# Bank waits at the output and merge products, an earlier remainder at the second index unit, head weights turned 72 rows at once, and row sums of the spatial weights in two fp32r parts

## The chip, the cores and the metric

The kernel runs on one core of one Trainium2 chip. The metric is the device time of one execution in microseconds, the median of several runs. TensorE (PE) multiplies, VectorE (DVE), ScalarE (ACT) and GpSimd (POOL) work element by element, SyncE (SP) issues the weight loads. Each engine runs its own list of instructions in order and waits on semaphores that the others raise.

## The reference, cut to what matters

Two blocks run one after the other on x of 256 rows by 1024 columns, all in float32:

```python
# first block
h = _rmsnorm(x, norm_g)
u, v, za, ab, ab_gate, zb, g_a, g_b = split(h @ w_in + b_in)          # 8 parts of 1024 columns
v = (_normalize(gelu(v)) * a_ln_g + a_ln_b)
mixed = einsum('gij,bnjgc->bnigc', masked(a_ws), v) + a_bs            # a_ws: 8 groups of 128 x 128
y_a = gelu(u) * mixed * silu(za)
y_b = silu(groupnorm(conv31(ab * sigmoid(ab_gate)))) * silu(zb)
merged = sigmoid(g_a) * (y_a @ w_pa) + sigmoid(g_b) * (y_b @ w_pb)
x = x + merged @ w_out
x = x + sigmoid(_rmsnorm(x, ple_norm_g) @ w_ple_gate) * (p @ w_ple)
x = _rmsnorm(x, final_g)
# second block
qa, ka, va, qb, kb, vb, qi, ki, wi, xc, yc, gates = split(_rmsnorm(x) @ w_in_2)
score = sum_h wi[h] * relu(qi[h] . ki)                                # 8 index heads, ki has 64 columns, wi has 8
y_a, y_b, y_c = attention, attention over the 64 best keys by score, gated linear recurrence
merged = g0 * (y_a @ w_pa_2) + g1 * (y_b @ w_pb_2) + g2 * (y_c @ w_pc_2)
x = x + merged @ w_o_2
x = x + relu(_rmsnorm(x) @ w_up_2)**2 @ w_down_2
return _rmsnorm(x, final_norm_g_2)
```

The bias a_ln_b of the layer norm goes through the spatial product as well: what it adds to row i of group g is a_ln_b times the sum of row i of the masked a_ws. These are the row sums of the title.

## The kernel before, in words

**Units.** All weights are cut into 123 units of 1 MB (some smaller), numbered c in the order of the list UNITS, which is written out by hand. A unit lands in one of three slots (c modulo 3) of `raw`. ScalarE copies it, rounded, to `whi` (`hi(c)`, L519, fp32r), and the remainder `raw - whi` goes to `wlo` (`lo(c)`, L897 on VectorE; for c from 3 to 27 both halves on GpSimd, L462). A product is then three fp32r matmuls for each k tile: high by high, high by low, low by high (L1547 to L1549). The inputs are held as such pairs too: a_hi and a_lo, b_hi and b_lo, c_hi and c_lo. Each engine's code walks the units; in the turn c ScalarE does `hi(c + 1)` or `hi(c + 2)` and drains the unit before.

**Banks.** The products of unit c go to PSUM bank U[c % 3]; M[0] to M[3] are four other banks and M[4] is an eighth. A bank is free for the next unit when the drain of its last user is counted in `act_drained` or `dve_drained`. `drained_count(c)` is the value of that counter once unit c has been drained.

**The places of the change.**
- Row sums (L1687 to L1690). After unit 8, the first v unit, TensorE multiplies the masked, transposed spatial weights wsT (8 groups of 128 columns) by a tile of ones into M[2] and M[3], as two fp32 matmuls of 512 columns. VectorE clears the masked corner of wsT in its turn c == 8 (L1009 to L1011). The sums are used in its turn c == 10 (L1015).
- Output (L1772 to L1774). The pb units are 36 to 39, in banks U[0], U[1], U[2], U[0]. The unit out 0 (`rows_half`) writes its rows 0 to 127 to U[2] and its rows 128 to 255 to U[0]. Before it, TensorE waits until unit 39 has been drained.
- Index units (L1218, L1292 to L1312). The units are qi 50 and 51, ki 52, xc 53 and 54. They are drained multiplied by r_bc, the reciprocal norm of each row, which TensorE spreads over the partitions in the middle of unit 53 (`norm_broadcast`, L1790) and VectorE copies to SBUF (L1218). Behind that copy VectorE does: drain qi 0, `lo(54)`, drain qi 1, `lo(55)`, drain ki, `lo(56)`, drain xc 0. TensorE may begin unit 54 only when qi 1, in its bank, has been drained; the first index scores (`dots`, L1802) want xc 0 drained.
- Head weights (L1869). Rows 64 to 71 of the ki product are wi. VectorE copies these 8 rows to wiT, and TensorE turns them into columns of M[2].
- Merge and w_o (L1938 to L1943). pb2 1 is unit 84 in U[0], pa2 0 and 1 are 85 in U[1] and 86 in U[2]. The unit wo 0 writes U[0] and U[1]; wo 1 writes U[2] and M[4]. Before wo 0 TensorE waits for the merged high and low parts (`m2_lo`) and until unit 86 has been drained.

Of the kernel before, what the change touches and what calls it, by code (L numbers as in the profile page):

```python
# [24 lines left out]
P = 128  # L25
# [104 lines left out]
def block_program(nc, I, onehot, causal, scratch, out):  # L130
    ctx = ExitStack()
    with ctx:
# [67 lines left out]
        gn_sq = reg_w[:, 0:1024].rearrange("p (t s) -> p t s", t=NT)  # L200
        bs_bc = reg_w[:, 1024:2048].rearrange("p (g i) -> p g i", g=KD)
# [45 lines left out]
        wiT = r8_bc[DH:DH + HEADS, :]  # L247
# [15 lines left out]
        def turned_tile(banks, k):  # L263
# [5 lines left out]
            in_lo xr_T xT_loaded pT_hi pT_lo wsT_sb rowsum_mm bs_ready  # L269
# [230 lines left out]
        def _(act):  # L500
# [82 lines left out]
            for c in range(1, FIRST["pa"] + 1):  # L583
# [9 lines left out]
                elif kind == "v" and j % 2:  # L593
                    act.wait_ge(Sm["multiplied"], c)
                    if j == 1:
                        act.wait_ge(Sm["xr_ready"], NR)
                    for r in range(NR):
                        act.activation(v_rows[:, r, S * (j - 1):S * (j + 1)], U[(c - 2 + r) % SLOTS][:, :],
                                       ACT.Gelu_apprx_tanh).then_inc(Sm["act_drained"], 1)
                elif kind == "u":  # L600
                    drain_tiles(c - 1, lambda n, j=j: u_act[:, 2 * j + n, :], ACT.Gelu_apprx_tanh, col)
                elif kind == "za":
                    drain_tiles(c - 1, tmp_tile(take_tmp()), ACT.Silu, col)
                elif kind == "zb":
                    drain_tiles(c - 1, lambda n, j=j: z_b[:, 2 * j + n, :], ACT.Silu, col)
                elif kind == "ga":
                    act.wait_ge(Sm["ya_lo"], j + 1)
                    drain_tiles(c - 1, lambda n, j=j: gate_a[:, 2 * j + n, :], ACT.Sigmoid, col)
                elif kind == "gb":
                    act.wait_ge(Sm["y_a"], j + 1)  # L610
                    drain_tiles(c - 1, lambda n, j=j: gate_b[:, 2 * j + n, :], ACT.Sigmoid, col)
                if c == 4:
# [264 lines left out]
        def _(ve):  # L877
# [117 lines left out]
            for c in range(1, FIRST["pa"] + 1):  # L995
# [13 lines left out]
                if c == 8:  # L1009
                    ve.wait_ge(Sm["early_loaded"], 64)  # L1010
                    ve.memset(wsT[64:P, :, 0:64], 0.0).then_inc(Sm["wsT_sb"], 1)  # L1011
                if c == 10:
# [203 lines left out]
            ve.tensor_scalar(rh_col[:, :], r_col, 0.5, None, ALU.mult).then_inc(Sm["rcol_ready"], 1)  # L1216
            ve.wait_ge(Sm["rbc_T"], 1)
# [65 lines left out]
            for c in range(FIRST["qi"] + 1, FIRST["pc2"] + 1):  # L1283
                kind, j = UNITS[c - 1]
                d = c - 1
                late = c + 2 > FIRST["xc"]
# [9 lines left out]
                elif kind == "ki":  # L1296
# [4 lines left out]
                    ve.tensor_copy(wiT, U[d % SLOTS][DH:DH + HEADS, 0:S]).then_inc(Sm["dve_drained"], 1)  # L1301
                elif kind == "xc":
                    if j == 0:
                        ve.memset(xc[:, :, 0:TAPS2 - 1], 0.0).then_inc(Sm["xcc_ready"], 1)
                    else:
                        ve.wait_ge(Sm["wi_T"], 1)
                        for r in range(NR):
                            ve.tensor_scalar(wi[:, r, :], M[2][:, HEADS * r:HEADS * (r + 1)], r_col[:, r:r + 1],
# [207 lines left out]
        def _(pe):  # L1516
# [159 lines left out]
            for c in range(FIRST["pa"]):  # L1676
# [9 lines left out]
                if c == 8:  # L1686
                    pe.wait_ge(Sm["wsT_sb"], 1)  # L1687
                    for h in range(2):
                        pe.matmul(M[2 + h][:, :], ones[:, :], wsT[:, 4 * h:4 * h + 4, :], start=True, stop=True
# [36 lines left out]
            def rows_half(c, banks, h, l, half_done=None, between=None):  # L1726
# [3 lines left out]
                for r in range(NR):  # L1730
                    ins = product(banks[r][:, :], row_tiles(h, l, r, KD // 2 * k_half),
                                  weights(c % SLOTS, KD // 2, 0, 2 * S), KD // 2, first=k_half == 0, last=k_half == 1)
                    if r == 0 and k_half == 1:
                        ins.then_inc(Sm[half_done], 1)
                        if between is not None:
                            between()
# [26 lines left out]
            pe.wait_ge(Sm["dve_drained"], drained_count(FIRST["pb"] + 3))  # L1763
            rows_half(OUT[0], out_bank[0], b_hi, b_lo)
# [90 lines left out]
            for c in range(FIRST["ki"], FIRST["pc2"]):  # L1855
# [10 lines left out]
                if c == FIRST["ki"] + 2:  # L1866
                    pe.wait_ge(Sm["dve_drained"], drained_count(FIRST["ki"]))
                    for r in range(NR):
                        ins = pe.transpose(M[2][:, HEADS * r:HEADS * (r + 1)], wiT[:, P * r:P * r + P],  # L1869
                                           ident[DH:DH + HEADS, DH:DH + HEADS])  # L1870
# [56 lines left out]
            pe.wait_ge(Sm["dve_drained"], drained_count(FIRST["pa2"] + 1))  # L1927
            rows_half(WO[0], wo_bank[0], b_hi, b_lo)
            merged_rows_T(1)
            rows_half(WO[1], wo_bank[1], b_hi, b_lo)  # L1930
# [118 lines left out]
```

## Time and profile before

| | |
|---|---|
| median of 3 runs | 759.66 us (759.6 to 760.16) |
| the profiled execution | 760.43 us |
| its span, first to last instruction | 758.6 us |
| TensorE busy | 743.4 us, 98% of the span |
| VectorE busy | 540.9 us, 71% |
| ScalarE busy | 393.2 us, 52% |
| GpSimd busy | 162.3 us, 21% |
| mean granted TensorE clock | 0.997 |

The span is the time that the trace covers; the device time also has some 1.8 us around it. TensorE is busy nearly all the time, so what counts is how much work it has and where it stands still.

### The profile page before, as it was taken

Reading aid. Unit: us, or ns where it says so; the run is one execution under the profiler, and the core shown is the slowest. Engines: PE = TensorE matmul, PEld = TensorE weight load, DVE = VectorE, ACT = ScalarE, POOL = GpSimd, SP = SyncE. Lnnn points to the kernel's source line nnn. Section 1 sums busy time; section 2 is a strip of 40 time slices with the busy share of each in tenths; the row PEclk is TensorE's granted clock in tenths of the full one; section 3 lists DMA queues with packets and bytes.
Section 4 is the critical chain, followed back from the end, with each engine's and each line's share of the span. In section 5 each row is a group of like instructions: output and inputs, shape, how many; then the busy total and the mean of one; then the engine's idle time right before and its main releaser. Section 6 shows DMA issues by size and latency. Waiting matters only on the chain.

```text
span 758.6 us, 11660 instructions
## 1 busy us (share of the span) xinstructions
PE 743.4 (98%) x4682; PEld 662.2 (87%) x4682; DVE 540.9 (71%) x865; ACT 393.2 (52%) x481; POOL 162.3 (21%) x99
## 2 busy tenths in 40 slices
PE   7999999999999999999999999999999999999996
PEld 7998999999999878989999777778789888888885
DVE  5394996999875786779897876565856655655664
ACT  6554544465553456753754555654436444454443
POOL 4799797972000000000021300000000000000000
PEclk9999999999999999999999999999999999999998
DMA  9866664556636597554556546446644566456521
GB/s 321 277 232 185 180 191 118 175 154 174 211 116 201 187 339 232 167 182 152 167 167 195 180 129 197 161 152 208 191 158 152 175 213 215 154 186 221 176 102 55
DMA packets 101266, 139.33 MB, mean 184 GB/s; under 512 B 4673, under 2 KB 75105, under 8 KB 101218
## 3 DMA queue, kind: packets, MB, share of 16 engines
q1 hardware_dynamic: 98242, 133.36, 54.4%
q10 hardware_dynamic: 2496, 3.73, 1.3%
q0 software_dynamic: 480, 1.57, 0.8%
q8 instruction: 34, 0.56, 0.3%
q14 instruction: 14, 0.11, 0.0%
HBM read 134.46 MB, written 4.19 MB: 183 GB/s over the span
## 4 chain that ended last, share of the span: by engine, by line
PE 86%; DVE 8%; issue 2%; ACT 2%; DMA 1%; POOL 1%; DVEq 0%; ACTq 0%
PE sums L1547 18%; PE sums L1548 17%; PE sums L1549 17%; PE sums L1942 7%; PE misc L1955 4%; PE misc L1957 4%; PE misc L1958 4%; PE sums L1944 4%; DVE sums L960 2%; PE misc L1518 2%; ACT s_whi L519 1%; DVE s_wlo L897 1%; PE sums L1588 1%; PE misc L1548 1%; PE misc L1549 1%
## 5 line engine op out<-in xcount | busy, mean ns | idle before, releaser
L519 ACT ACTIVATE s_whi<-s_raw 128x2048 fp32r<-128x2048 f32 x93 | 174.6, 1880 | 87.6 <-PE sums L1549 54.0
L897 DVE TENSOR_TENSOR s_wlo<-s_raw,s_whi 128x2048 fp32r<-128x2048 f32 (+2 forms) x68 | 150.1, 2209 | 64.5 <-ACT s_whi L519 64.0
L1547 PE MATMUL sums<-s_a_parts,s_whi 128*128 128x256 f32 x496 | 141.1, 285 | 0.1
L1549 PE MATMUL sums<-s_a_parts,s_wlo 128*128 128x256 f32 x496 | 140.6, 283 | 0.0
L1548 PE MATMUL sums<-s_a_parts,s_whi 128*128 128x256 f32 x496 | 140.6, 283 | 0.0
L462 POOL TENSOR_TENSOR s_wlo<-s_raw,s_whi 128x1024 fp32r<-128x1024 f32 x52 | 128.9, 2506 | 26.4 <-ACT s_whi L519 26.4
L1547 PEld LDWEIGHTS sums<-s_a_parts,s_whi 128*128 128x128 f32 x496 | 95.3, 192 | 0.8 <-issue 0.7
L1548 PEld LDWEIGHTS sums<-s_a_parts,s_whi 128*128 128x128 f32 x496 | 95.3, 192 | 0.1
L1549 PEld LDWEIGHTS sums<-s_a_parts,s_wlo 128*128 128x128 f32 x496 | 95.3, 192 | 0.0
L960 DVE SCALAR_TENSOR_TENSOR sums<-s_reg_d,s_vectors,sums 128x256 f32<-128x256 f32 x232 | 92.6, 477 | 0.0
L835 ACT ACTIVATE s_whi<-s_raw 128x2048 fp32r<-128x2048 f32 x29 | 55.6, 1919 | 63.6 <-PE sums L1944 50.2
L1942 PE MATMUL sums<-s_a_parts,s_whi 128*128 128x512 f32 x240 | 85.3, 399 | 0.0
L1547 PE MATMUL sums<-s_whi,s_b_hi 128*128 128x512 f32 x192 | 77.2, 402 | 2.1 <-issue 0.8
L1548 PE MATMUL sums<-s_wlo,s_b_hi 128*128 128x512 f32 x192 | 75.1, 391 | 0.0
L1549 PE MATMUL sums<-s_whi,s_b_lo 128*128 128x512 f32 x192 | 74.9, 390 | 0.0
L1547 PE MATMUL sums<-s_b_hi,s_whi 128*128 128x256 f32 (+1 forms) x248 | 71.3, 288 | 1.3 <-DVE s_reg_d L1065 1.3
L1548 PE MATMUL sums<-s_b_lo,s_whi 128*128 128x256 f32 (+1 forms) x248 | 70.3, 283 | 0.0
L1549 PE MATMUL sums<-s_b_hi,s_wlo 128*128 128x256 f32 (+1 forms) x248 | 70.2, 283 | 0.0
L1944 PE MATMUL sums<-s_a_parts,s_wlo 128*128 128x256 f32 x240 | 67.5, 281 | 0.0
L1486 DVE TENSOR_TENSOR s_wlo<-s_raw,s_whi 128x2048 fp32r<-128x2048 f32 x29 | 66.1, 2288 | 1.2 <-ACT s_whi L835 1.1
L1942 PEld LDWEIGHTS sums<-s_a_parts,s_whi 128*128 128x128 f32 x240 | 45.2, 188 | 10.9
L1955 PE MATMUL misc<-s_whi,s_b_hi 128*128 128x512 f32 x128 | 50.1, 391 | 0.0
(318 smaller groups left out, 1370.2 us busy)
## 6 DMA issues: line engine op xcount, KB each, us to landing
s_raw<-in_w_in SPq DMA_DIRECT2D x61, 1024.0 KB, 5.8
s_raw<-in_w_up SPq DMA_DIRECT2D x16, 1024.0 KB, 5.5
s_raw<-in_w_down SPq DMA_DIRECT2D x16, 1024.0 KB, 6.4
s_raw<-in_w_pa SPq DMA_DIRECT2D x6, 1024.0 KB, 5.1
s_raw<-in_w_pb SPq DMA_DIRECT2D x6, 1024.0 KB, 5.7
s_raw<-in_w_out SPq DMA_DIRECT2D x4, 1024.0 KB, 5.1
s_raw<-in_w_ple_gate SPq DMA_DIRECT2D x4, 1024.0 KB, 6.7
s_raw<-in_w_o SPq DMA_DIRECT2D x4, 1024.0 KB, 5.1
```

The source lines that it names most:

```text
L462: gp.tensor_tensor(wlo[:, c % SLOTS, cols], raw[:, c % SLOTS, cols], whi[:, c % SLOTS, cols].bitcast(F32), ALU.subtract).then_inc(Sm["pool ...
L519: act.activation(ring_view(whi, c), ring_view(raw, c), ACT.Copy).then_inc(Sm["hi_ready"], 1)
L835: act.activation(whi[:, slot, :], raw[:, slot, :], ACT.Copy).then_inc(Sm["hi_ready"], 1)
L897: ve.tensor_tensor(dst, src, part.bitcast(F32), ALU.subtract).then_inc(Sm["lo_ready"], 1)
L960: ve.scalar_tensor_tensor(dst, h_pad[:, t, k:k + S], col(w_conv, k * KD + t), acc, ALU.mult, ALU.add).then_inc(Sm["tap"], 1)
L1486: ve.tensor_tensor(wlo[:, n % SLOTS, :], raw[:, n % SLOTS, :], whi[:, n % SLOTS, :].bitcast(F32), ALU.subtract).then_inc(Sm["lo_ready"], 1)
L1547: pe.matmul(dst, sh, mh, start=first and k == 0, stop=False)
L1548: pe.matmul(dst, sh, ml, start=False, stop=False)
L1549: ins = pe.matmul(dst, sl, mh, start=False, stop=last and k == kt - 1)
L1942: pe.matmul(bank.rearrange("p (b s) -> p b s", b=2), wh, a_parts[:, :, k, :], start=k == 0, stop=False, skip_group_check=True)
L1944: ins = pe.matmul(bank[:, 0:S], wl, a_hi[:, k, :], start=False, stop=k == KD - 1, skip_group_check=True)
L1955: pe.matmul(M[n][:, :], hh, wh[:, k, cols], start=first and k == 0, stop=False, skip_group_check=True)
```

## The change

It has five parts. The row sums are made from two fp32r parts of wsT: ScalarE rounds wsT to wsT_hi (in b_hi[4:8], turn c == 7), VectorE writes the remainder wsT_lo (in b_lo[4:8], turn c == 8), and TensorE does four fp32r matmuls in place of two fp32 ones; the clearing of the corner moves to the turn c == 6. The wait for unit 39 at out 0 stands between its two halves of rows, with a wait for unit 38 before the first. `lo(54)` comes before the copy of r_bc in place of behind the drain of qi 0. The head weights are turned as 72 rows, from partition 0. At wo 0 the wait is for unit 85; the one for unit 86 comes after the second half of the merged rows has been turned, before wo 1.

```diff
@@ ScalarE
+                if c == 7:
+                    act.wait_ge(Sm["wsT_sb"], 1)
+                    act.activation(wsT_hi, reg_w[:, 0:1024].rearrange("p (t s) -> p t s", t=4), ACT.Copy
+                                   ).then_inc(Sm["wsT_hi"], 1)
@@ VectorE
-                if c == 8:
+                if c == 6:
                     ve.wait_ge(Sm["early_loaded"], 64)
                     ve.memset(wsT[64:P, :, 0:64], 0.0).then_inc(Sm["wsT_sb"], 1)
+                if c == 8:
+                    ve.wait_ge(Sm["wsT_hi"], 1)
+                    split_lo(wsT_lo, reg_w[:, 0:1024].rearrange("p (t s) -> p t s", t=4), wsT_hi, "wsT_lo")
...
+            lo(FIRST["xc"] + 1)
             ve.wait_ge(Sm["rbc_T"], 1)
             ve.tensor_copy(r_bc[:, :], M[4][:, 0:S]).then_inc(Sm["rb_ready"], 1)
...
-                late = c + 2 > FIRST["xc"]
+                late = c + 2 > FIRST["xc"] + 1
...
-                    ve.tensor_copy(wiT, U[d % SLOTS][DH:DH + HEADS, 0:S]).then_inc(Sm["dve_drained"], 1)
+                    ve.tensor_copy(wiT, U[d % SLOTS][0:DH + HEADS, 0:S]).then_inc(Sm["dve_drained"], 1)
@@ TensorE
-                    pe.wait_ge(Sm["wsT_sb"], 1)
+                    pe.wait_ge(Sm["wsT_lo"], 1)
                     for h in range(2):
-                        pe.matmul(M[2 + h][:, :], ones[:, :], wsT[:, 4 * h:4 * h + 4, :], start=True, stop=True
+                        four = slice(2 * h, 2 * h + 2)
+                        pe.matmul(M[2 + h][:, :], ones_r, wsT_hi[:, four, :], start=True, stop=False)
+                        pe.matmul(M[2 + h][:, :], ones_r, wsT_lo[:, four, :], start=False, stop=True
                                   ).then_inc(Sm["rowsum_mm"], 1)
...
-                        if between is not None:
-                            between()
+                    if r == 0 and between is not None:
+                        between()
...
-            pe.wait_ge(Sm["dve_drained"], drained_count(FIRST["pb"] + 3))
-            rows_half(OUT[0], out_bank[0], b_hi, b_lo)
+            pe.wait_ge(Sm["dve_drained"], drained_count(FIRST["pb"] + 2))
+            rows_half(OUT[0], out_bank[0], b_hi, b_lo,
+                      between=lambda: pe.wait_ge(Sm["dve_drained"], drained_count(FIRST["pb"] + 3)))
...
-                        ins = pe.transpose(M[2][:, HEADS * r:HEADS * (r + 1)], wiT[:, P * r:P * r + P],
-                                           ident[DH:DH + HEADS, DH:DH + HEADS])
+                        ins = pe.transpose(M[2][:, P * r:P * r + DH + HEADS], wiT[:, P * r:P * r + P],
+                                           ident[0:DH + HEADS, 0:DH + HEADS])
...
             pe.wait_ge(Sm["m2_lo"], 2)
-            pe.wait_ge(Sm["dve_drained"], drained_count(FIRST["pa2"] + 1))
+            pe.wait_ge(Sm["dve_drained"], drained_count(FIRST["pa2"]))
             rows_half(WO[0], wo_bank[0], b_hi, b_lo)
             merged_rows_T(1)
+            pe.wait_ge(Sm["dve_drained"], drained_count(FIRST["pa2"] + 1))
             rows_half(WO[1], wo_bank[1], b_hi, b_lo)
```

On TensorE, at the end of unit 8, the kernel before has two matmuls of 512 columns that read the spatial weights in s_reg_w:

```order
L1548 MATMUL sums<-s_wlo,s_a_parts 128x512
L1549 MATMUL sums<-s_whi,s_a_parts 128x512
L1689 MATMUL misc<-s_reg_w,s_ones 128x512 [waits wsT_sb]
L1689 MATMUL misc<-s_reg_w,s_ones 128x512
L1547 MATMUL sums<-s_whi,s_a_parts 128x512 [waits act_drained,pool_lo_ready,lo_ready]
```

In the changed kernel there are four, which read the two parts in s_b_hi and s_b_lo:

```order
L1557 MATMUL sums<-s_wlo,s_a_parts 128x512
L1558 MATMUL sums<-s_whi,s_a_parts 128x512
L1699 MATMUL misc<-s_b_hi,s_ones 128x512 [waits wsT_lo]
L1700 MATMUL misc<-s_b_lo,s_ones 128x512
L1699 MATMUL misc<-s_b_hi,s_ones 128x512
L1700 MATMUL misc<-s_b_lo,s_ones 128x512
L1556 MATMUL sums<-s_whi,s_a_parts 128x512 [waits act_drained,pool_lo_ready,lo_ready]
```

The wait moved from the clearing of the corner to the remainder, and the two fp32 matmuls have become four fp32r ones.

On VectorE, in its turns 5 to 9, the kernel before has the clearing (MEMSET) between the convolution's taps (L960):

```order
L900 TENSOR_TENSOR s_b_hi<-s_reg_f,s_b_hi 1x1024 [waits bv_hi]
L960 SCALAR_TENSOR_TENSOR sums<-s_reg_d,s_vectors,sums 128x256 [waits tap] x27
L1011 MEMSET s_reg_w 64x8x64 [waits early_loaded]
L960 SCALAR_TENSOR_TENSOR sums<-s_reg_d,s_vectors,sums 128x256 [waits tap] x15
L960 SCALAR_TENSOR_TENSOR s_abc<-s_reg_d,s_vectors,sums 128x256 [waits tap] x2
```

The changed kernel clears 18 taps sooner and has the subtraction for wsT_lo where the clearing was:

```order
L905 TENSOR_TENSOR s_b_hi<-s_reg_f,s_b_hi 1x1024 [waits bv_hi]
L965 SCALAR_TENSOR_TENSOR sums<-s_reg_d,s_vectors,sums 128x256 [waits tap] x9
L1016 MEMSET s_reg_w 64x8x64 [waits early_loaded]
L965 SCALAR_TENSOR_TENSOR sums<-s_reg_d,s_vectors,sums 128x256 [waits tap] x18
L905 TENSOR_TENSOR s_b_lo<-s_reg_w,s_b_hi 128x1024 [waits wsT_hi]
L965 SCALAR_TENSOR_TENSOR sums<-s_reg_d,s_vectors,sums 128x256 [waits tap] x15
```

One subtraction of 128x1024 is added in front of the last taps of this stretch.

On VectorE at the index units, the kernel before copies r_bc, drains qi 0 (the first s_reg_d row), makes the remainder of unit 54, and only then drains qi 1:

```order
L1216 TENSOR_SCALAR s_rh_col<-s_r_col 128x2
L1218 COPY s_r_bc<-sums 128x256 [waits rbc_T]
L1065 TENSOR_TENSOR s_reg_d<-sums,s_r_bc 128x512 [waits multiplied,rb_ready]
L897 TENSOR_TENSOR s_wlo<-s_raw,s_whi 128x2048 [waits hi_ready]
L1065 TENSOR_TENSOR s_reg_d<-sums,s_r_bc 128x512 [waits multiplied]
L897 TENSOR_TENSOR s_wlo<-s_raw,s_whi 128x2048 [waits hi_ready]
L1299 TENSOR_TENSOR s_reg_d<-sums,s_r_bc 64x256 [waits multiplied]
L1299 TENSOR_TENSOR s_reg_d<-sums,s_r_bc 64x256
L1301 COPY s_r_bc<-sums 8x256
```

In the changed kernel the same rows stand in this order:

```order
L1224 TENSOR_SCALAR s_rh_col<-s_r_col 128x2
L902 TENSOR_TENSOR s_wlo<-s_raw,s_whi 128x2048 [waits hi_ready]
L1227 COPY s_r_bc<-sums 128x256 [waits rbc_T]
L1073 TENSOR_TENSOR s_reg_d<-sums,s_r_bc 128x512 [waits multiplied,rb_ready]
L1073 TENSOR_TENSOR s_reg_d<-sums,s_r_bc 128x512 [waits multiplied]
L902 TENSOR_TENSOR s_wlo<-s_raw,s_whi 128x2048 [waits hi_ready]
L1308 TENSOR_TENSOR s_reg_d<-sums,s_r_bc 64x256 [waits multiplied]
L1308 TENSOR_TENSOR s_reg_d<-sums,s_r_bc 64x256
L1310 COPY s_r_bc<-sums 72x256
```

The remainder of unit 54 moved in front of the copy, the two qi drains stand side by side, and the copy of the head weights has 72 rows.

## Rows read from the trace of the kernel before

**Rows 1.** Waits of TensorE over the whole span: us in total, times, longest.

```profile
PE misc L1518 <- DMA s_abc<-in_x: 4.7, 1, 4.7
PE sums L1547 <- DVE s_reg_d L1065: 1.3, 1, 1.3
PE sums L1547 <- issue: 0.8, 1, 0.8
...
PE sums L1547 <- DVE s_tmp L1065: 0.6, 1, 0.6
```

**Rows 2.** Timeline of TensorE at the row sums: start, duration, count, idle before.

```profile
64.30 0.40 PE L1549 MATMUL sums<-s_whi,s_a_parts 128*128 128x512 f32 x1
64.53 1.88 PE L1689 MATMUL misc<-s_reg_w,s_ones 128*128 128x512 f32 x4
...
66.48 0.40 PE L1548 MATMUL sums<-s_wlo,s_a_parts 128*128 128x512 f32 x1
```

**Rows 3.** Timeline of VectorE, 55.3 to 73.1 us.

```profile
55.39 0.48 DVE L1011 MEMSET s_reg_w<- 64x512 f32 x1 [0.16 <-issue]
...
73.03 0.43 DVE L1002 BATCH_NORM_STATS2 s_bn<-s_abc 128x6 f32<-128x256 f32 x1 [10.00 <-ACT s_abc L598]
```

**Rows 4.** Timeline of GpSimd, 53 to 74 us.

```profile
52.86 9.51 POOL L462 TENSOR_TENSOR s_wlo<-s_raw,s_whi 128x1024 fp32r<-128x1024 f32 x4
...
63.57 9.45 POOL L462 TENSOR_TENSOR s_wlo<-s_raw,s_whi 128x1024 fp32r<-128x1024 f32 x4
```

**Rows 5.** Timeline of all engines around 44 us, where a VectorE subtraction meets GpSimd's.

```profile
41.17 5.75 POOL L462 TENSOR_TENSOR s_wlo<-s_raw,s_whi 128x1024 fp32r<-128x1024 f32 x2
41.24 3.40 DVE L900 TENSOR_TENSOR s_b_hi<-s_reg_f,s_b_hi 1x1024 fp32r<-1x1024 f32 x1
```

**Rows 6.** Timeline of all engines at the start of out 0.

```profile
257.25 2.29 DVE L897 TENSOR_TENSOR s_wlo<-s_raw,s_whi 128x2048 fp32r<-128x2048 f32 x1 [1.11 <-ACT s_whi L519]
...
259.25 0.39 PE L1549 MATMUL misc<-s_whi,s_c_lo 128*128 128x512 f32 x1
259.47 0.68 DVE L1065 TENSOR_TENSOR s_tmp<-sums,s_abc 128x512 f32<-128x512 f32 x1
...
260.25 0.47 PE L1547 MATMUL sums<-s_whi,s_b_hi 128*128 128x512 f32 x1 [0.61 <-DVE s_tmp L1065]
```

**Rows 7.** Timeline of VectorE at the index units.

```profile
329.18 0.42 DVE L1218 COPY s_r_bc<-sums 128x256 f32<-128x256 f32 x1 [2.85 <-PE sums L1790]
...
330.24 2.28 DVE L897 TENSOR_TENSOR s_wlo<-s_raw,s_whi 128x2048 fp32r<-128x2048 f32 x1
332.44 0.68 DVE L1065 TENSOR_TENSOR s_reg_d<-sums,s_r_bc 128x512 f32<-128x512 f32 x1
```

**Rows 8.** Timeline of ScalarE at the same place.

```profile
325.63 3.70 ACT L519 ACTIVATE s_whi<-s_raw 128x2048 fp32r<-128x2048 f32 x2
```

**Rows 9.** Timeline of TensorE at the start of unit 54.

```profile
331.73 0.28 PE L1549 MATMUL misc<-s_b_hi,s_wlo 128*128 128x256 f32 x1
333.27 0.36 PE L1547 MATMUL sums<-s_b_hi,s_whi 128*128 128x256 f32 x1 [1.26 <-DVE s_reg_d L1065]
```

**Rows 10.** Timeline of all engines at the first index scores.

```profile
338.89 0.69 DVE L1065 TENSOR_TENSOR s_reg_s<-misc,s_r_bc 128x512 f32<-128x512 f32 x1
...
339.19 0.29 PE L1869 MATMUL misc<-s_ident,s_r_bc 8*128 8x8 f32 x2
...
339.64 0.49 PE L1802 MATMUL misc<-s_reg_d 64*128 64x256 f32 x2 [0.16 <-DVE s_reg_s L1065]
```

**Rows 11.** Timeline of VectorE at the merge.

```profile
546.84 1.28 DVE L1392 SCALAR_TENSOR_TENSOR s_b_lo<-misc,s_b_hi 128x512 fp32r<-128x512 f32 x2
...
548.97 0.69 DVE L1410 SCALAR_TENSOR_TENSOR s_tmp<-s_abc,misc 128x512 f32<-128x512 f32 x1 [0.25 <-PE misc L1549]
```

**Rows 12.** Timeline of TensorE at the start of wo 0.

```profile
548.54 0.39 PE L1549 MATMUL misc<-s_whi,s_a_parts 128*128 128x512 f32 x1
549.75 0.47 PE L1547 MATMUL sums<-s_whi,s_b_hi 128*128 128x512 f32 x1 [0.82 <-issue]
```

More of the change, by code:

```diff
@@ L200, in block_program @@
         gn_sq = reg_w[:, 0:1024].rearrange("p (t s) -> p t s", t=NT)
+        wsT_hi, wsT_lo = b_hi[:, 4:8, :], b_lo[:, 4:8, :]
         bs_bc = reg_w[:, 1024:2048].rearrange("p (g i) -> p g i", g=KD)
@@ L246, in block_program @@
         sel_bc = c_lo[:, 2:4, :].rearrange("p a (t m) -> p (a t) m", m=P)
-        wiT = r8_bc[DH:DH + HEADS, :]
+        wiT = r8_bc[0:DH + HEADS, :]
         sp = sb("sp", [P, 8, NT])
@@ L268, in block_program @@
             ssq_ready rinv_ready rstd_ready xr_ready first_loaded first_hi first_lo in_hi
-            in_lo xr_T xT_loaded pT_hi pT_lo wsT_sb rowsum_mm bs_ready
+            in_lo xr_T xT_loaded pT_hi pT_lo wsT_sb wsT_hi wsT_lo rowsum_mm bs_ready
             h_ready tap conv_mean d_ready gsq_ready gvar_ready gstd_ready grcp_ready gbc_ready
@@ L1307, in _ @@
                         for r in range(NR):
-                            ve.tensor_scalar(wi[:, r, :], M[2][:, HEADS * r:HEADS * (r + 1)], r_col[:, r:r + 1],
+                            ve.tensor_scalar(wi[:, r, :], M[2][:, P * r + DH:P * r + DH + HEADS], r_col[:, r:r + 1],
                                              None, ALU.mult).then_inc(Sm["wi_ready"], 1)
```

## The prediction

> **What bounds the kernel now.** I read the busy table first: TensorE has matmuls in flight for 743.4 us of a span of 758.6. The next view is its list of waits [rows 1]. It holds 4.7 us at the start for the input, and beyond that only single waits of 1.3, 0.8 and 0.6 us in places that the change touches: 1.3 for a drain into s_reg_d (the qi units), 0.8 put down to "issue", and 0.6 for a drain into s_tmp (the pb units). The kernel is bound by TensorE's list, so a time can be won in two ways only: less work in that list, or one of these waits. Each is therefore read from the timeline around its own place. I count from the start of the matmul before a gap to the start of the one after it, less the step that two such matmuls have with no gap, since the end of a matmul is modelled. That step is 64.53 - 64.30 = 0.23 us for 512 columns [rows 2], and half of that, 0.12, for 256.
>
> **Row sums.** From the start of L1689 at 64.53 to the second matmul of unit 9 at 66.48 are 1.95 us [rows 2]. Less the 0.23 of unit 9's first matmul, the two fp32 matmuls (four records) cost 1.72. Four fp32r matmuls of the same 512 columns are priced by their like, 4 x 0.23 = 0.92. The gain is **0.80 us**, if the parts are there in time.
>
> Two instructions are added. ScalarE rounds 128x1024, half the size of its unit copies of 1.85 us each [rows 8], so some 0.93 us. It stands between unit 6's drain and the copy of unit 9, about 54 to 55 us. VectorE subtracts 128x1024. The nearest row is the same operation with one row of 1024 elements, 3.40 us at 41.24 while GpSimd was at work [rows 5]; with GpSimd idle, half the 2.28 us of 128x2048 [rows 7], 1.14. It comes at about 55.8, in the place of the clearing at 55.39 [rows 3], and so is done by 57.0 at the best and 59.2 at the worst. TensorE asks for it at 64.53, at least 5 us later. What is queued behind it on VectorE are the taps of turns 8 and 9, and behind them VectorE stood idle for 10.00 us until 73.03 [rows 3]. An extra 1.1 to 3.4 us vanish in that hole. Without the hole they would go to the taps, and by them to the group norm. The moved clearing (0.48) is paid and saved inside the same stretch.
>
> GpSimd is the cover that is thinner. In [rows 5] it took 5.75 us for two subtractions that take 9.51 / 2 = 4.76 in [rows 4], 1.0 more, while VectorE's own ran to 44.64, 1.1 after GpSimd's first (2.38) would have ended: the two don't overlap. So GpSimd is to slip by 1.0 to 1.2 us. Its work for unit 9 ends at 52.86 + 9.51 = 62.4, for units 10 and 11 at 68.3 and 73.0 [rows 4]. TensorE begins unit 9 at 66.25 - 0.80 = 65.45, and the two after it, at 24 x 0.23 = 5.5 us or more each, at 70.9 and 76.4. The slack is 3.1, 2.6 and 3.4 us, more than the slip. I take it as hidden. The Trainium skill, "SBUF — State Buffer", section "SBUF: two separate sides", says the same of the pair and speaks against this edit: a VectorE instruction with two SBUF inputs and a GpSimd instruction that reads SBUF hold the shared port as an exclusive lock, and the later one waits for the whole of the other. By that rule the slip repeats only where the instructions meet, once here; the trace's 1.0 us agrees.
>
> **Out 0.** The matmul before it starts at 259.25, so TensorE would go on at 259.48; it goes on at 260.25 [rows 6]. What it waits for is unit 39's drain, 259.47 + 0.68 = 260.15, so a released engine starts 0.10 after the end. In the new order this drain is needed only by the second half, 12 x 0.23 = 2.8 us later. But the remainder of unit 41 itself, which the first half needs, ends at 257.25 + 2.29 = 259.54 [rows 6]. The start goes to 259.64. The gain is 260.25 - 259.64 = **0.61 us** of the 0.77 in the gap.
>
> **Index units.** Unit 54 could start at 331.73 + 0.12 = 331.85 and starts at 333.27 [rows 9], 0.83 after the start of qi 1's drain at 332.44 [rows 7]. New order on VectorE: `lo(54)` waits for ScalarE's first copy, half of 3.70 behind 325.63, some 327.5 [rows 8], and takes 332.44 - 330.24 = 2.20 to the next instruction [rows 7]: 329.75. The copy of r_bc, ready for VectorE at 329.18 until now, is 0.57 late. Copy and drain of qi 0 take 330.24 - 329.18 = 1.06 together, so the drain of qi 1 starts at 330.81, 1.63 sooner than 332.44. TensorE is released at 330.81 + 0.83 = 331.64, 0.2 before it is ready. So the wait goes to zero, and unit 54 starts 1.42 sooner.
>
> What is late next is the drain of xc 0, in front of the first index scores: they start at 339.64, 0.16 us of it waiting [rows 10]. `lo(55)`, the ki drains, `lo(56)` and that drain follow qi 1's without a gap, so it moves by 1.63 as well, to 337.26, and releases TensorE at 338.01. TensorE's own list gets to the turned head weights at 339.19 - 1.42 = 337.77 and needs 0.29 for them as 8 columns [rows 10], so 338.06. The 72 columns are not in the trace. Below: nothing, if the two are bound by their latency. Above: 2 x 64 columns at fp32's 1.72 us per 1024 columns [rows 2], 0.22 us. I take 0.04, the near end, since 0.29 for 8 columns is plainly not a matter of columns. The scores start at 338.10; the gain is 339.64 - 338.10 = **1.54 us** (1.36 to 1.58). The copy of 72 rows in place of 8 costs nothing on an engine where all partitions work side by side. The load of unit 57, which waits for `lo(54)`, leaves 2.7 us sooner, so the copy behind it is no new brake.
>
> **Wo 0.** The matmul before it starts at 548.54, so it could start at 548.77; it starts at 549.75 [rows 12]. The profile says "issue", but the drain of unit 86's second half ends at 548.97 + 0.69 = 549.66 [rows 11], 0.09 before: this is the wait that is moved. The other condition, the two merged remainders, ends at 546.84 + 1.28 = 548.12 [rows 11] and with 0.10 releases at 548.22, before 548.77. The gain is the whole **0.98 us**. The moved wait comes after some 5.5 us of wo 0 and the transposes, long after the drain.
>
> **The sum.** 0.80 + 0.61 + 1.54 + 0.98 = 3.93 us. All four are in TensorE's own list, and the engines behind it mostly wait for TensorE, so I let them add. The profiled execution has 760.43 us with a span of 758.6; it should become 756.5 with 754.7. The median of the runs shown is 759.66, 0.77 below it, and becomes **755.7 us**.
>
> **The rivals.**
> - *One of the two large gaps stays* (chance 0.22). At the index units the margin is 0.2 us: a remainder that starts 0.5 later takes back 0.3. At wo 0 the word "issue" speaks for a cause of TensorE's own; then 0.98 is lost, and the sum is 2.95: 756.7. Without the 1.54 it is 2.4: 757.3. Against it: both gaps close within 0.1 us of the drain's end.
> - *The gains are eaten downstream* (0.08). Around out 0 VectorE and ScalarE pass `hi`, `lo` and merge to and fro, and that chain does not move with TensorE; the remainder that is ready only at 259.54 is its sign [rows 6]. If a later remainder holds TensorE in the same way, the 0.61 and what came before it are given back, and the sum falls below 1.5: 758.5 to 759.7. Against it: [rows 1] has no wait for a remainder.
> - *GpSimd's lock costs more* (0.03). If GpSimd slips at unit 10 by more than 2.6 us, TensorE stands in the v units and the 0.80 is lost: 756.5.
> - *Slower* (0.04). `lo(54)` now stands in front of the copy of r_bc, behind ScalarE's copy of unit 54, and everything at the index units waits for r_bc. Each us by which that copy ends after 327.5 goes one to one to TensorE once 0.2 is used up. It decides when it ends after 333.1, 5.6 later: then unit 54 starts at 331.64 + 5.6 = 337.24, 4.0 us later than now in place of 1.42 sooner, more than the other 2.4 us by 1.6, and the kernel takes 761.3 us. Against it: the two copies in [rows 8] run back to back with no wait for a load in them.
> - *The forecast* (0.63): a sum between 3.4 and 4.5 us.
>
> **How the numbers follow.** A measurement tells this kernel from itself down to some 0.2%, 1.5 us. Faster by more than that are the forecast, the first rival and the lock: 0.63 + 0.22 + 0.03 = 0.88. Within 0.2% is the second rival, 0.08; slower 0.04. The range takes the forecast's 755.2 to 756.3 and the first rival's 756.7 to 757.3. It needs some room, since the 759.66 comes from three runs that differ by 0.56 us: **754.6 to 757.7**.
>
> **What would show it.** The changed kernel's list of TensorE's waits should have lost the 1.3, the 0.8 and all but 0.2 of the 0.6. The four row-sum matmuls should take 0.92 us. The copy of r_bc should be later than the end of its matmul by 0.6, and the two s_reg_d drains stand 0.6 apart. GpSimd should show one subtraction that is 1.0 to 1.2 longer near 57 us, and VectorE a hole of 6 to 9 us in place of 10.00. I am wrong if unit 54 still waits for a drain, if wo 0 still waits with no releaser, or if a wait for a remainder (L897) or for GpSimd appears.

## The result and the profile after

The changed kernel takes **755.94 us** (median of 5 runs, 755.7 to 756.24), the kernel before 760.03 (median of 5) on the same chip: a ratio of 0.9945, 95% interval 0.9934 to 0.9956. The forecast was 755.7 in 754.6 to 757.7. The span went from 758.6 to 754.3 us, TensorE's busy time from 743.4 to 741.8, and the mean granted clock is 0.998.

The list of TensorE's waits in the changed kernel (us in total, times, longest):

```profile
PE misc L1527 <- DMA s_abc<-in_x: 4.7, 1, 4.7
PE sums L1556 <- DVE s_reg_w L1299: 0.7, 1, 0.7
PE sums L1597 <- DVE s_a_parts L938: 0.2, 1, 0.2
PE misc L1671 <- ACT s_reg_w L571: 0.2, 1, 0.2
```

Beside [rows 1], the 1.3, the 0.8 and the 0.6 are gone. The 0.7 for s_reg_w is an old one, at 432 us; it was in the kernel before too (experiment 6).

The row sums, on TensorE's timeline (start, duration; as in [rows 2]):

```profile
64.52 0.39 PE L1699 MATMUL misc<-s_b_hi,s_ones 128*128 128x512 f32 x1
...
65.22 0.40 PE L1700 MATMUL misc<-s_b_lo,s_ones 128*128 128x512 f32 x1
65.45 0.39 PE L1556 MATMUL sums<-s_whi,s_a_parts 128*128 128x512 f32 x1
65.68 0.39 PE L1557 MATMUL sums<-s_wlo,s_a_parts 128*128 128x512 f32 x1
```

From the first of them to unit 9's second matmul are 65.68 - 64.52 = 1.16 us, in place of 1.95. What it costs GpSimd and VectorE, on their timelines (as in [rows 3, 4]):

```profile
52.83 10.50 POOL L463 TENSOR_TENSOR s_wlo<-s_raw,s_whi 128x1024 fp32r<-128x1024 f32 x4
...
64.53 9.49 POOL L463 TENSOR_TENSOR s_wlo<-s_raw,s_whi 128x1024 fp32r<-128x1024 f32 x4
```

```profile
55.82 2.88 DVE L905 TENSOR_TENSOR s_b_lo<-s_reg_w,s_b_hi 128x1024 fp32r<-128x1024 f32 x1
...
72.22 1.08 DVE L1007 BATCH_NORM_STATS2 s_bn<-s_abc 128x6 f32<-128x256 f32 x3 [6.40 <-ACT s_abc L599]
```

GpSimd's four subtractions take 10.50 in place of 9.51, all of it in one of them (3.40 from 57.57, for 2.41), and the next four start 0.96 later; TensorE's list has no wait for them. VectorE's hole is 6.40 us long.

Out 0, on the timelines of VectorE and TensorE (as in [rows 6]):

```profile
256.34 2.29 DVE L902 TENSOR_TENSOR s_wlo<-s_raw,s_whi 128x2048 fp32r<-128x2048 f32 x1 [1.11 <-ACT s_whi L520]
```

```profile
258.41 0.39 PE L1558 MATMUL misc<-s_whi,s_c_lo 128*128 128x512 f32 x1
258.78 0.47 PE L1556 MATMUL sums<-s_whi,s_b_hi 128*128 128x512 f32 x1
```

The step of 0.37 holds a gap of 0.14, and out 0 starts 0.15 after unit 41's remainder ends at 258.63.

The index units, on VectorE's timeline (as in [rows 7]) and TensorE's (as in [rows 9, 10]):

```profile
326.08 2.29 DVE L902 TENSOR_TENSOR s_wlo<-s_raw,s_whi 128x2048 fp32r<-128x2048 f32 x1 [1.24 <-ACT s_whi L520]
328.29 0.42 DVE L1227 COPY s_r_bc<-sums 128x256 f32<-128x256 f32 x1
328.75 1.29 DVE L1073 TENSOR_TENSOR s_reg_d<-sums,s_r_bc 128x512 f32<-128x512 f32 x2
```

```profile
330.25 0.28 PE L1558 MATMUL misc<-s_b_hi,s_wlo 128*128 128x256 f32 x1
330.37 0.28 PE L1556 MATMUL sums<-s_b_hi,s_whi 128*128 128x256 f32 x1
...
336.01 0.29 PE L1558 MATMUL sums<-s_b_hi,s_wlo 128*128 128x256 f32 x1
336.14 0.29 PE L1881 MATMUL misc<-s_ident,s_r_bc 72*128 72x72 f32 x2
```

Unit 54 follows unit 53 with the plain step of 0.12. At w_o (as in [rows 12]):

```profile
545.27 0.39 PE L1558 MATMUL misc<-s_whi,s_a_parts 128*128 128x512 f32 x1
545.49 0.39 PE L1556 MATMUL sums<-s_whi,s_b_hi 128*128 128x512 f32 x1
```

Wo 0 follows without a gap as well.

To see where the time came from I pair the matmuls of two traces by their number, 4682 in each, and follow the difference of their starts; each place where it jumps is a step. From before to after: row sums +0.80, out 0 +0.63, unit 54 +1.50, head weights and first scores +0.31, wo 0 +1.07. With 0.07 of other small offsets these are 4.38 us at the last matmul. In what follows "a step" is meant in this way.

### The profile page after: what moved, and what is told of

Same layout as the page of the kernel before. It is cut to its first block, busy times and chain, and to the rows that moved or that the text cites. A ratio compares the mean times of both kernels' runs of the same rounds, so it can differ in the third digit from the quotient of the medians.

```text
span 754.3 us, 11663 instructions
## 1 busy us (share of the span) xinstructions
PE 741.8 (98%) x4682; PEld 661.9 (88%) x4682; DVE 543.3 (72%) x866; ACT 394.2 (52%) x482; POOL 163.3 (22%) x99
## 4 chain that ended last, share of the span: by engine, by line
PE 92%; DVE 5%; POOL 1%; ACT 1%; DMA 1%; issue 0%; DVEq 0%; ACTq 0%
PE sums L1556 19%; PE sums L1557 18%; PE sums L1558 18%; PE sums L1955 7%; PE misc L1968 4%; PE misc L1970 4%; PE misc L1971 4%; PE sums L1957 4%; DVE sums L965 2%; PE misc L1527 2%; PE misc L1556 1%; PE misc L1557 1%; PE misc L1558 1%; PE sums L1597 1%; PE sums L1593 1%; PE sums L1595 1%
## 5 line engine op out<-in xcount | busy, mean ns | idle before, releaser
L902 DVE TENSOR_TENSOR s_wlo<-s_raw,s_whi 128x2048 fp32r<-128x2048 f32 (+2 forms) x68 | 150.1, 2208 | 65.9 <-ACT s_whi L520 65.3
```

Of the source, the lines that this page charges most:

```text
L902: ve.tensor_tensor(dst, src, part.bitcast(F32), ALU.subtract).then_inc(Sm["lo_ready"], 1)
```

## The experiments

"Profiled span" is that of one execution; spans of one kernel differ by 0.3 us from the start of the program alone, so the steps tell more. All medians stand beside the kernel before at 760.03 to 760.30.

**1. Parts alone.** Into the kernel before goes the row-sum part alone (e1: the edits of ScalarE, VectorE and TensorE for wsT_hi and wsT_lo), or the two bank waits alone (e4):

```diff
-            pe.wait_ge(Sm["dve_drained"], drained_count(FIRST["pb"] + 3))
+            pe.wait_ge(Sm["dve_drained"], drained_count(FIRST["pb"] + 2))
...
+                      between=lambda: pe.wait_ge(Sm["dve_drained"], drained_count(FIRST["pb"] + 3)))
...
-            pe.wait_ge(Sm["dve_drained"], drained_count(FIRST["pa2"] + 1))
+            pe.wait_ge(Sm["dve_drained"], drained_count(FIRST["pa2"]))
...
+            pe.wait_ge(Sm["dve_drained"], drained_count(FIRST["pa2"] + 1))
```

> The kernel before with the row-sum edit alone (two fp32r parts, added ScalarE copy and VectorE subtraction). Theory (each part frees its own time in TensorE's list and nothing behind it takes it back): the span falls from 758.6 to 757.8 us, 0.80 less; out 0 and unit 54 keep their gaps of 0.77 and 1.42 us; VectorE's subtraction takes some 2.9 us beside GpSimd, and GpSimd slips by 1.0. Rival (the chain between VectorE and ScalarE around out 0 does not move with TensorE): the gap before out 0 grows from 0.77 to about 1.6 us and the span stays at 758.6.

> The kernel before with the two bank waits moved alone (out 0 and wo 0). Theory: out 0 starts 0.6 us sooner, wo 0 1.0 sooner, the span falls by 1.6 to 1.7 us to 757.0; unit 54 keeps its gap of 1.42. Rival (the word issue at wo 0 stands for a cause of TensorE's own): only the 0.6 comes, the span is 758.0, and the idle time before wo 0 is still 0.8.

Measured: e1 759.24 us (ratio 0.9988, 0.9979 to 0.9998), with a step of +0.80 at the row sums that lasts to the end. But there was also +0.49 at out 0, whose wait e1 does not touch. e4 took 758.58 (0.9979, 0.9969 to 0.9988), with steps of +0.85 at out 0 and +1.07 at wo 0; the gap at unit 54 stayed. The row sums and wo 0 are as predicted and need no other part. Out 0 needed a better explanation (experiment 4).

**2. The changed kernel without one part.** e2 puts the remainder of unit 54 back behind the drain of qi 0:

```diff
-            lo(FIRST["xc"] + 1)
...
-                late = c + 2 > FIRST["xc"] + 1
+                late = c + 2 > FIRST["xc"]
```

e3 copies and turns the head weights as 8 rows from partition 64:

```diff
-                    ve.tensor_copy(wiT, U[d % SLOTS][0:DH + HEADS, 0:S]).then_inc(Sm["dve_drained"], 1)
+                    ve.tensor_copy(wiT, U[d % SLOTS][DH:DH + HEADS, 0:S]).then_inc(Sm["dve_drained"], 1)
...
-                        ins = pe.transpose(M[2][:, P * r:P * r + DH + HEADS], wiT[:, P * r:P * r + P],
-                                           ident[0:DH + HEADS, 0:DH + HEADS])
+                        ins = pe.transpose(M[2][:, HEADS * r:HEADS * (r + 1)], wiT[:, P * r:P * r + P],
+                                           ident[DH:DH + HEADS, DH:DH + HEADS])
```

> The changed kernel with the remainder of unit 54 back behind the drain of qi 0; everything else as changed. Theory (this move closes the wait at the start of unit 54): the gap of 1.42 us is back there, the first index scores wait for xc 0 again, and the span grows from 754.3 to about 755.9, 1.6 more. Rival (the 72-row turning did the main part at the index units): the span grows by less than 0.8 us.

> The changed kernel with the head weights copied and turned as 8 rows from partition 64 again. Theory A (the 8 rows from partition 64 cost time at three steps: the start of the turning matmuls, and the copy on VectorE that holds the next instruction back): the first index scores come 0.2 to 0.3 us later against the start of unit 54, the span is 754.55. Theory B (as the prediction had it, the size is all but free and the extra 0.26 us have another source): the span stays at 754.3 within 0.05 and the first scores keep their 5.99 us behind the start of unit 54.

Measured: e2 757.73 us (0.9969, 0.9958 to 0.9981), the wait of 1.3 is back, and the index units give +0.25 in place of +1.81. The early remainder is worth 1.56. e3: 756.43 (0.9952, 0.9936 to 0.9969); its index units give +1.62. So 72 rows are 0.19 better than 8, where I had allowed a cost. (The 0.22 in the expectation that follows was a first reading of the same steps.)

**3. Whose are those 0.19?** e7 keeps the copy of 72 rows and turns 8:

```diff
...
-                        ins = pe.transpose(M[2][:, P * r:P * r + DH + HEADS], wiT[:, P * r:P * r + P],
-                                           ident[0:DH + HEADS, 0:DH + HEADS])
+                        ins = pe.transpose(M[2][:, HEADS * r:HEADS * (r + 1)], wiT[DH:DH + HEADS, P * r:P * r + P],
+                                           ident[DH:DH + HEADS, DH:DH + HEADS])
```

> The changed kernel, with VectorE's copy of 72 rows kept, but TensorE turns only the 8 rows of the head weights, from partition 64 to 71. The step from the last matmul of unit 54 to the first index score was 0.35 us with 72 rows turned (336.01 to 336.36) and 0.66 in the kernel before, where 0.16 of it was a wait. Theory A, the 0.22 us is on TensorE's side: with 8 rows the step is 0.5 or more again, and no wait stands in it. Theory B, the 0.22 us came from VectorE, whose copy of 8 rows took 0.45 us to the next instruction and that of 72 rows 0.34, so that the drain in front of the scores came sooner: then the step stays at 0.35 to 0.40. The span is no test of it, since it varies by 0.3 from run to run (754.0 to 754.8 in either case).

Measured: 755.8 us, one run. Neither theory: the step from unit 54's last matmul to the first score is 0.42, between the 0.35 of the changed kernel (336.36 - 336.01) and 0.54 in e3. TensorE in e7 and in e3:

```profile
335.68 0.28 PE L1558 MATMUL sums<-s_b_hi,s_wlo 128*128 128x256 f32 x1
335.89 0.29 PE L1881 MATMUL misc<-s_ident,s_r_bc 8*128 8x8 f32 x2
336.10 0.49 PE L1814 MATMUL misc<-s_reg_d 64*128 64x256 f32 x2
```

```profile
335.94 0.28 PE L1558 MATMUL sums<-s_b_hi,s_wlo 128*128 128x256 f32 x1
336.15 0.29 PE L1881 MATMUL misc<-s_ident,s_r_bc 8*128 8x8 f32 x2
336.48 0.49 PE L1814 MATMUL misc<-s_reg_d 64*128 64x256 f32 x2
```

The turning of 8 rows starts 0.21 behind the last matmul in both, that of 72 rows 0.13: 0.08 of the difference is TensorE's. The other 0.11 stands between the turning and the score (0.33 in e3, 0.21 in e7, 0.22 in the changed kernel). There e3's score comes 0.75 after the start of xc 0's drain, as in the kernel before [rows 10]: it waits for VectorE. VectorE in e3, then in the changed kernel:

```profile
332.93 0.42 DVE L1310 COPY s_r_bc<-sums 8x256 f32<-8x256 f32 x1
333.38 2.29 DVE L902 TENSOR_TENSOR s_wlo<-s_raw,s_whi 128x2048 fp32r<-128x2048 f32 x1
335.63 0.07 DVE L1313 MEMSET s_reg_s<- 128x12 f32 x1
335.73 0.69 DVE L1073 TENSOR_TENSOR s_reg_s<-misc,s_r_bc 128x512 f32<-128x512 f32 x1
```

```profile
333.00 0.42 DVE L1310 COPY s_r_bc<-sums 72x256 f32<-72x256 f32 x1
333.34 2.28 DVE L902 TENSOR_TENSOR s_wlo<-s_raw,s_whi 128x2048 fp32r<-128x2048 f32 x1
335.56 0.67 DVE L1073 TENSOR_TENSOR s_reg_s<-misc,s_r_bc 128x512 f32<-128x512 f32 x1
335.57 0.07 DVE L1313 MEMSET s_reg_s<- 128x12 f32 x1
```

Behind the copy of 72 rows the remainder starts 0.08 before the copy's end (333.42), behind that of 8 rows 0.03 after it (333.35); and the drain of xc 0 starts beside the clearing in one and behind it in the other. From copy to drain are 2.56 us against 2.80. The Trainium skill, "VectorE: DVE Perf Modes", section "Two Vector instructions with no wait between them", says that an instruction waits for all earlier ones on VectorE where its output starts in another group of 32 partitions than the last output in the same memory, or its input in another than the last input. The copy of 8 rows reads and writes from partition 64; the remainder behind it writes from 0, and the drain of xc 0 is the next to read PSUM, from 0. By that rule both places would be held with 8 rows and free with 72; the trace agrees at both. No run copies or turns 8 rows from partition 0, so the runs alone do not tell the number of rows from the partition that they start at.

**4. What sets the gap at out 0.** It was 0.77 in the kernel before and 0.28 in e1 with the same wait, 0.14, 0.06, 0.00 and 0.00 with the new one. e9 makes ScalarE's copies of units 39 to 42 one step earlier, each before the rounding of the merged part that it stood behind:

```diff
+            hi(FIRST["pb"] + 2)
...
-                hi(FIRST["pb"] + 2 + j)
+                hi(FIRST["pb"] + 3 + j)
...
-            hi(FIRST["out"] + 1)
```

> The changed kernel, with ScalarE's copies of units 38 to 41 one unit further ahead of its rounding of the merged parts. In the five kernels run so far the gap before out 0 was 0.77, 0.28, 0.14, 0.06, 0.00 and 0.00 us by run, and it followed the time at which ScalarE copied unit 38 (16.70, 16.21, 16.63, 16.55, 16.44 and 16.17 us behind a fixed matmul) more than the edit. Theory: the chain of copy, remainder and merge behind that load is what sets out 0's start, so with the copies earlier the gap is 0.00 to 0.05 whatever the load does; span 0.1 to 0.2 below the changed kernel's, which is less than a measurement tells (ratio 0.9985 to 1.0005 against the changed kernel by medians). Rival: a merged part then reaches TensorE late, since the copy stands in front of it, and a wait for b_hi or b_lo of up to 1.9 us (one copy) shows up before or in out 0; span 755 to 756.

> The changed kernel once more, beside the two others on one chip. Theory: what varies between its executions is the gap at out 0, which follows the arrival of unit 38's load (gap = start of ScalarE's copy of it behind TensorE's matmul 1650, less 16.49 us, where positive) and the start of the program (0.3 us). So a median of 755.7 to 756.3, and in the profiled execution a gap that fits the relation within 0.1 us. Rival: the gap and the start of the copy do not fit each other (more than 0.2 us off), and the relation found over nine traces was chance.

(The values in the first of these are of six kernels, the one before among them.) Measured: e9 755.82 us (0.9937, 0.992 to 0.9953), no gap at out 0, no wait for b_hi or b_lo; its time cannot tell it from the changed kernel's, as expected. e12, the changed kernel again: 756.03 us (755.63 to 757.39), and its profiled execution had a gap of 1.22, as the relation foretells (17.71 - 16.49). TensorE there, and ScalarE's copy of unit 38:

```profile
258.68 0.39 PE L1558 MATMUL misc<-s_whi,s_c_lo 128*128 128x512 f32 x1
260.13 0.47 PE L1556 MATMUL sums<-s_whi,s_b_hi 128*128 128x512 f32 x1 [1.06 <-DVE s_wlo L902]
```

```profile
239.31 1.91 ACT L520 ACTIVATE s_whi<-s_raw 128x2048 fp32r<-128x2048 f32 x1 [8.91 <-DMA s_raw<-in_w_pb]
```

All traces, by the start of that copy behind TensorE's matmul 1650 (at 222.17 in the kernel before):

| kernels | copy of unit 38, us | gap at out 0, us |
|---|---|---|
| wait for unit 39: before, e1 | 16.70, 16.21 | 0.77, 0.28 |
| new wait: after, e2, e6 | 16.63, 16.55, 16.78 | 0.14, 0.06, 0.29 |
| new wait: e8, e12 | 17.55, 17.71 | 1.06, 1.22 |
| new wait: e3, e4, e7, e11 | 16.44, 16.17, 16.23, 16.25 | 0.00 |
| new wait, copies ahead: e9, e10 | 16.61, 16.74 | 0.00 |

The gap is the copy's start less 15.93 with the old wait and less 16.49 with the new one, and none where that is negative, in every trace without copies ahead to 0.01. (The 15.93 rests on two traces.) So out 0's start hangs on a chain that begins when unit 38's load lands (ScalarE waits for it in the row above, and starts 0.02 to 0.03 after the landing in all traces). Its links behind that, copies, drains, merges and remainders, are read from the code; e9's edit of the copies shortens it. The new wait lets out 0 start 0.56 us sooner on this chain. What a run shows at out 0 is that, more or less what the load does. With the copies ahead, a load as late as that of the kernel before gives no gap.

**5. The rival "slower" in small.** e6 puts a second remainder in front of the copy of r_bc; e11 is the same kernel, timed:

```diff
             lo(FIRST["xc"] + 1)
+            lo(FIRST["xc"] + 2)
             ve.wait_ge(Sm["rbc_T"], 1)
...
-                late = c + 2 > FIRST["xc"] + 1
+                late = c + 2 > FIRST["xc"] + 2
```

> The changed kernel, with the remainder of unit 55 as well in front of the copy of r_bc: the rival 'slower' of the prediction in small. The prediction's theory: everything that stands in front of that copy goes one to one to TensorE once the margin is used up. VectorE would make the second remainder at 328.28 to 330.5, copy r_bc at 330.5 in place of 328.29 and start the drain of qi 1 near 331.6 in place of 329.4; TensorE is released 0.83 later, at 332.4, and the changed kernel starts unit 54 at 330.37. So a wait of 1.9 to 2.0 us for the s_reg_d drain is back in front of unit 54, and the span goes from 754.3 to 756.3, the time to some 757.9. Rival: VectorE has slack at this place, because the remainder of unit 55 has to be made sooner or later anyway and the drains are not what TensorE waits for; then less than 0.5 us is lost (span below 754.8).

> The kernel with both remainders in front of the copy of r_bc, timed. Its one look showed more than the wait: the wait of 1.85 us, and from 1.5 us behind it TensorE at a granted clock of 0.50 (1.2 of 2.4 GHz) for some 3.3 us, which cost 1.5 us more; span 757.9 in place of 756.3. Theory: the fall of the clock belongs to the wait, so it comes in most executions, and the median lies 3.4 to 3.9 us above the changed kernel's. Rival: the fall was an accident of that one execution; then the median lies 1.9 to 2.3 us above it and the new profile shows a clock of 1.00 behind the wait.

Measured: e6 759.66 us in its one run, span 757.9; e11 758.66 (757.86 to 759.63, ratio 0.9979). TensorE in e6 at unit 54, and the windows behind it (length, busy time of PE, PEld, DVE, ACT, POOL, granted clock, DMA share, GB/s):

```profile
332.45 0.36 PE L1557 MATMUL sums<-s_b_hi,s_whi 128*128 128x256 f32 x1 [1.85 <-DVE s_reg_d L1073]
```

```profile
331.00:334.00 3.00, 1.54 (x13) 1.58 (x14) 2.95 (x6) 1.61 (x1) 0.00 (x0) 1.00 1.09 369
334.00:336.00 2.00, 2.00 (x12) 2.00 (x11) 2.00 (x3) 0.00 (x0) 0.00 (x0) 0.50 1.05 329
336.00:338.00 2.00, 2.00 (x14) 2.00 (x13) 0.31 (x1) 0.00 (x0) 0.00 (x0) 0.65 0.52 122
338.00:341.00 3.00, 3.00 (x28) 2.76 (x27) 0.00 (x0) 0.97 (x1) 0.00 (x0) 1.00 0.77 269
```

The wait is what the prediction's slope gives: unit 54 starts at 332.45 for an expected 332.4, a step of -2.08 against the changed kernel. But there is a second loss. Some 1.5 us after TensorE goes on, its granted clock falls from 1.00 to 0.50 (from 2.4 to 1.2 GHz) for 3.4 us, and the same matmuls start 0.21 apart in place of 0.12. That takes 1.48 us more (steps of -0.37 for each four matmuls). The profile of e11 (759.36 us) shows the fall again, here 0.4 us after TensorE goes on, for 3.4 us and 1.48 us by its steps, with out 0 without a gap.

Shorter waits left the clock at 1.00. From the start of the last matmul before the wait to the first one after it are 2.13 us in e6 and e11; they are 1.54 at the same place in the kernel before [rows 9], e1, e2 and e4, and 1.45 at out 0 in e12, and in none of these five traces does the clock fall between the start of the program and its end.

The ten runs of e11 lie in two groups of five, 757.86 to 758.13 and 759.19 to 759.63. The median of the ten, 2.63 above the changed kernel's, is what neither theory foretold. The lower group is 2.0 above it, which is the wait alone. That its clock stayed up, and that it fell in the four unprofiled runs of the upper group, is inferred from the times and from the mean granted clock of the runs (0.9982 in the lower group, 0.9966 in the upper; a fall of 3.4 us to 0.50 is worth 0.0023). A late load of unit 38 could lift single runs as well. So the fall comes in about half of the executions, by inference.

**6. The last wait in TensorE's list.** e8 moves a product of the recurrence behind the va drains:

```diff
+                if c == SCAN_AT + 4:
+                    ve.wait_ge(Sm["lru_dve"], 3)
+                    ve.wait_ge(Sm["yc_act"], 2)
+                    ve.tensor_tensor(lru_a, lru_r, yc, ALU.mult).then_inc(Sm["lru_dve"], 1)
                 if late:
...
-                elif c == SCAN_AT + 3:
-                    ve.wait_ge(Sm["lru_dve"], 3)
-                    ve.wait_ge(Sm["yc_act"], 2)
-                    ve.tensor_tensor(lru_a, lru_r, yc, ALU.mult).then_inc(Sm["lru_dve"], 1)
```

> The changed kernel, with one product of the recurrence (128x1024, 1.21 us at 430.45) moved behind the two va drains that TensorE waits for at 431.58. Theory of the prediction, carried to the last wait that is left in TensorE's list (0.7 us for s_reg_w): TensorE's list is the bound and a wait that a VectorE order makes is won in full. The drains start 1.13 us sooner, the wait of 0.7 goes away, and VectorE has an idle 0.41 us behind the drains in which a part of the product is absorbed. Span 753.6 to 753.8, time 0.65 us below the changed kernel's. Rival: the moved product makes the remainder behind it late (433.39 now), and TensorE waits for that in place of the drain; then a wait for L902 shows up and the span stays at 754.1 to 754.5.

> The changed kernel with both edits that were tried alone: the product of the recurrence behind the va drains, and ScalarE's copies of units 38 to 41 one further ahead. Theory, from the two traces: the first took a gap away that was worth 0.96 us by the starts of the matmuls (offset to the changed kernel -0.94 before it, +0.05 behind it), but its own execution lost 0.95 at out 0, where unit 38's load came late; the second keeps out 0 without a gap although its load came 0.12 us later than the latest one that gives none. Together: no wait at out 0 in any execution, none at the va drains, span 753.0 to 753.4, median 1.0 to 1.3 us below that of the changed kernel in the same call. Rival: the two depend on each other or the gain at the va drains is given back behind it (a wait for a remainder near 433); then the span stays at 754.0 or above and the medians differ by less than 0.4 us.

Measured: e8 755.39 us (754.83 to 755.99, ratio 0.9929). Its profiled span of 754.2 alone would have read as "no gain", and one wait for L902 is in its list; but that wait is at out 0 (0.9, the load of unit 38 again), not behind the drains, where the step is +0.97. That is more than the 0.65 expected, since the list's 0.7 was taken as the gap: in the changed kernel the matmuls around it start 1.08 apart, a gap of 0.85, and the restart behind it takes 0.12 more. Both edits together, e10: **754.87 us** (754.61 to 755.07, five runs; ratio to before 0.9928, 0.9915 to 0.9942), 1.16 below the changed kernel timed beside it (756.03), span 753.1. TensorE's waits in e10, and its first matmul behind the va drains:

```profile
PE misc L1527 <- DMA s_abc<-in_x: 4.9, 1, 4.9
PE misc L1671 <- ACT s_reg_w L571: 0.3, 1, 0.3
PE sums L1597 <- DVE s_a_parts L938: 0.2, 1, 0.2
```

```profile
431.11 0.39 PE L1558 MATMUL sums<-s_whi,s_b_lo 128*128 128x512 f32 x1
431.34 0.39 PE L1556 MATMUL sums<-s_whi,s_b_hi 128*128 128x512 f32 x1
```

Behind the 4.9 us at the start, no wait above 0.3 us is left in TensorE's list. The runs are also closer together, 0.46 us from lowest to highest against 1.76 in e12. That a load as late as e12's would no longer show is not proved by this: no trace of e9 or e10 has one later than 16.74.

## Why the prediction was right, step by step

- *What bounds the kernel.* TensorE's list did, as every step shows. But the list of waits was read with a line too few. Beside the 1.3, 0.8 and 0.6 it held this one, which the change does not touch:

```profile
PE sums L1547 <- DVE s_reg_w L1290: 0.7, 1, 0.7
```

So it is wrong that all waits behind the first stand in places that the change touches. The sum does not use this one, so the forecast did not suffer; e8 and e10 show that it was worth 0.97.

- *Row sums, 0.80.* Measured +0.80, in the changed kernel and alone. VectorE's subtraction took 2.88, within 1.1 to 3.4, and went into the hole (10.00 to 6.40). GpSimd slipped by 0.96 to 0.99, for a forecast of 1.0 to 1.2, and once only; the rival of the lock fell. The lengths fit two engines that take turns: GpSimd's subtraction from 55.20 ends at 57.62, and from there to the end of VectorE's at 58.70 are 1.08, near the 1.14 estimated for it alone.
- *Out 0, 0.61.* Measured +0.63. The step was right, and its limit, the remainder of unit 41, was named. That the sizes agree so well is in part luck: both ends of the gap move with unit 38's load, which the prediction did not see. At the load time of the kernel before (16.70) the new wait leaves 0.21 of 0.77 and the edit is worth 0.56; in e12 there was a gap of 1.22 in spite of it. The rival "eaten downstream" named the right chain, and in e12 the step at out 0 was -0.45, which took back more than half of the 0.80 of the row sums. That was the load: with an early one, e1 kept its 0.80 and the gap shrank to 0.28. The rival's price was also wrong by its own terms, since 0.61 and 0.80 given back leave 2.52, 757.1 us, and not a sum below 1.5.
- *Index units, 1.54.* Measured 1.81, the term that was mis-sized most, by 0.27. Of it 0.08 is the restart: a first matmul behind a wait takes 0.20 to the next in place of 0.12, so a removed wait gives the gap and that. Another 0.08 is the turning, which starts 0.13 behind the last matmul in place of 0.21. The last 0.11 is the way from the turning to the first score, 0.22 where 0.29 + 0.04 = 0.33 was foretold. Both of these come with the 72 rows (experiment 3), which I took as a cost. "Below: nothing" was the wrong lower bound.
- *Wo 0, 0.98.* Measured +1.07, again with the restart; alone +1.07 too. The word "issue" in the profile stood for VectorE's drain, as its end 0.09 before the start said, and e4 shows it: the gap goes when the wait for that drain is moved.
- *The sum, 3.93.* 4.38 by the steps, 4.09 between the medians of the runs timed together. The terms add: the steps at the row sums, the index units and wo 0 are the same to 0.02 us in every kernel that has the edit whole.
- *The rivals.* No large gap stayed. "Slower" was right in its slope: the second remainder cost 2.08 us for 2.03 foretold. Its point of decision was set too late, since it counted no fall of the clock. Where the clock falls, with 1.48 more, a copy of unit 54 that ends about 4.1 us later would have done it, in place of 5.6; this is an estimate from e6 and e11.

## What to carry to other kernels

In a kernel bound by one engine's list, each wait in that list is worth its gap (read from start to start, not from the list) and the 0.08 to 0.12 us of the restart, and the timeline around it tells which instruction's end it follows, whatever name the list of waits gives. Before a term is booked from one trace, look whether the gap hangs on a chain that starts with a load: then its size is a matter of the execution, and the edit's worth is the shift of the relation, not the difference of two gaps. And a profiled span can hide a gain of 1 us behind such a load, so take the steps place by place.

## What the hardware showed unexpectedly

- A wait of 1.8 to 1.9 us of TensorE was followed by a granted clock of 0.50 for 3.4 us, in both profiled executions (e6, e11) and, by inference from the times, in about half of ten runs. Waits of 1.26 and 1.27 at the same place, in four traces, were not.
- Copying 72 rows from partition 0 leaves VectorE free earlier than copying 8 rows from partition 64: 2.56 against 2.80 us from the copy to the drain of xc 0. Turning 72 rows starts 0.08 us sooner on TensorE than turning 8 from partition 64.
- The load of unit 38, 1 MB issued behind seven small ones, came up to 1.5 us later in one execution than in another (copies at 16.17 to 17.71 us behind the same matmul). The first of the seven is issued 5.84 to 5.85 us behind that matmul in all traces. Unit 38's is issued at 10.30 to 11.03, and lands 5.5 to 6.1 us after that in all traces but e8 and e12, where it takes 6.8 and 7.2. Why was not tried.
